# A two-layer decoder step: the mLSTM gates' scans moved into the first projection, and the mixer's start and the output projection's start reordered

## The chip, the core and the metric

The kernel runs on one core of one Trainium2 chip. The metric is the device time of one execution, in microseconds (us). The median of three runs of the kernel before is 2627.14 us (2625.72 to 2627.63). Profiled once, it took 2626.53 us.

## The reference, cut to what matters

Layer 0 has four mLSTM heads and four retention heads, each 256 wide, for a prompt of 1024 tokens and 8 sample sequences of 4 tokens ("samples"). One input projection gives q, k, v and a gate path z of every head, and for the mLSTM heads two scalars a token, ig and fg. Everything that the weights of a chunk need from these scalars depends on ig, fg and the old m alone:

```
p = h @ w_in
qk_m, v_m, z_m, ig, fg, q_r, k_r, v_r, z_r = split(p)
qk_c = silu(conv(buf0, qk_m))                  # conv_p, conv_s: the last rows
hm, C, n, m = mlstm_scan(q_m, k_m, v_m, ig + b_i, fg + b_f, C0, n0, m0)
    b = cumsum(log_sigmoid(fg))                # scans along the tokens
    Dm = b[t] - b[s] + ig[s];  m_t = maximum(b + m, max(Dm))
    w = exp(Dm - m_t)                          # weights of q k^T
    ws = exp(bL - b + ig - m_new);  sc = exp(bL + m - m_new)
hr, S = retention_scan(rope(q_r), rope(k_r), v_r, S0)
out = concat(rms(hm) * silu(z_m), rms(hr) * silu(z_r)) @ w_out
```

Layer 1 is differential attention, in stages that the change leaves alone.

## The kernel before

The program is a list of stages, each with one program per engine: norm, `project_layer0` (p0), `mix` (mx), `project_out_a` (oa), the second projection, attention and the last projection. Engines hand the memory over at a stage's end by the semaphores `left` and `cleared`.

**project_layer0** loops over 8 heads, mLSTM heads 0 to 3 and retention heads 4 to 7 (`head_loop`). For a head, TensorE (PE) computes four column tiles of q and k (`tile`, L572 to L574, about 11 us each) and the row blocks of v and z (`row_block`) in the order tile 0, tile 1, row block 1, tile 2, row blocks 2 and 3, tile 3, row blocks 4 to 8. Tile j lies in PSUM buffer j modulo 2, and PE takes a buffer again when `tile_taken` says so:

```
pe.wait_ge(tile_taken, m * 4 + (j + 1))        # tile(m, j)
dve.wait_ge(raw_ready, m * 4 + (2 * pair + 2)) # rotate(m, h, pair), heads 4 to 7
dve.sem_inc(tile_taken, 2)
```

ScalarE (ACT) copies a tile from PSUM (L680, L681), and VectorE (DVE) does the convolution of an mLSTM head or the rotation of a retention head (`rotate`, from L884 on). Results go to DRAM (`s_qk`, `s_v`, `s_g`) and come back in the mixer. Nearly all DMAs are issued by SyncE (SP), in the order of its program; it issues the next only when the queue has taken the last. The gate scalars (`s_gates`) are stored before the first head. The last rows of the convolution (`conv_p`, `conv_s`) are stored at the stage's end.

**mix** begins with the gates' chain (L1487 to L1522: scans on 4 partitions, by DVE, with an exponential and a logarithm of ACT within it, L1396 and L1398), then four exponentials (L1400 to L1402 and one more). PE turns the results into columns (L1229), spreads the samples' gates (L1237 to L1241), prepares the first chunk (`spread_m` L1249 and L1255, `turn_k` L1285, `scores` L1268), and then runs 8 chunks of 128 tokens, each with its products (`mx_num` L1311, L1340 to L1342) and one piece of the samples' work, beginning with `t_num(0)` (L1307), which needs the samples' values `t_v` and, for its later part, their state `t_state` (`load_t`). POOL clears the state (`mx_state`, L1469) and then signals `ready`, for which ACT and DVE wait and through them `gates_done`.

**project_out_a** multiplies the mixed rows by `w_out`. For the first row block b = 0, PE takes the 16 slices k one by one as ACT and DVE split them (`w_split`), and puts `project_few(k + 2)` (L1843, the samples' rows) between. For a row block it first turns the rows `oa_y` (`turn_y`, L1826). SP meanwhile has the final states to store (`store_states`: C_p, S_p, n_p, the last rows of `s_y`, n_s).

Of the kernel before, what the change touches and what calls it, by code (L numbers as in the profile page):

```python
# [31 lines left out]
P = 128  # L32
# [7 lines left out]
H = 4  # L40
# [329 lines left out]
def project_layer0(c, h_hi, h_lo, h_few):  # L370
# [9 lines left out]
    with Stage(c, "p0") as st:  # L380
# [50 lines left out]
        def head_loop(eng, body):  # L431

            with eng.Fori(0, H) as m:
                body(m, m, True)
            with eng.Fori(H, HEADS) as m:
                body(m, m - H, False)
# [38 lines left out]
        def sync(sp):  # L475
# [185 lines left out]
        def scalar(act):  # L661
# [36 lines left out]
            def body(m, h, mlstm):  # L698
# [5 lines left out]
                take_rows(m, 1)  # L704
                if mlstm:
                    sigmoid_exp(m, 1)
# [17 lines left out]
            head_loop(act, body)  # L724
# [69 lines left out]
        def vector(dve):  # L794
# [134 lines left out]
            head_loop(dve, body)  # L929
# [14 lines left out]
def mix(c, nxt):  # L944
# [8 lines left out]
    with Stage(c, "mx") as st:  # L953
# [12 lines left out]
        rows = st.sb("rows", [H, 2, NT], at=1664)  # L966
# [3 lines left out]
        t_q = st.sb("t_q", [P, 2, 2, DB, S], at=207488)  # L970
        t_w = st.sb("t_w", [S, 2, 4, S], at=211584)
        n_old = st.sb("n_old", [P, 2, S], at=212608)
        n_new = st.sb("n_new", [P, 2, S], at=212864)
        n_inc = st.sb("n_inc", [P, 2, S], at=213120)
        t_hn = st.sb("t_hn", [P, HH, VX], at=213376)
        places = {"late": 221600, "early": 162784}
# [6 lines left out]
        t_rep = little("t_rep", "late", [S, 2, P])  # L983
        n_out = st.sb("n_out", [S, DK], at=221600)
        select = little("select", "late", [H, H, P])
        junk = little("junk", "late", [P, 2, DK])
        n_rows = little("n_rows", "late", [S, DK])
        t_qw = little("t_qw", "late", [P, HH, S])
        mask = little("mask", "late", [P, P])
        t_wz = little("t_wz", "late", [P, HH, 2])  # L990
        t_wt = little("t_wt", "early", [S, HH, S])
# [3 lines left out]
        ws_rows = little("ws_rows", "early", [H, S])  # L995
# [14 lines left out]
        gates = st.sb("gates", [H, 2, NT], at=27264)  # L1010
        b = st.sb("b", [H, NT], at=35712)
        zeros = st.sb("zeros", [H, P], at=39936)
        ones = st.sb("ones", [H, P], at=40448)
        em = st.sb("em", [H, NT], at=10112)
        ws = st.sb("ws", [H, NT], at=14336)
        a = st.sb("a", [H, NT], at=20128)
        M = st.sb("M", [H, NT], at=92896)
        reset = st.sb("reset", [H, NT], at=121664)
        NCH = NB + DB
        small = {}  # L1020
        at = 18560
# [46 lines left out]

        def sync(sp):
# [69 lines left out]
            sp.wait_ge(gates_done, 1)  # L1139
# [85 lines left out]
        def tensor(pe):  # L1225
            pe.wait_ge(gr_dve, 2)
            for n in range(NB + 1):
                for q, x in ((A, a), (EM, em), (WS, ws)):
                    pe.transpose(pt[0:rows_of(n), (n * 3 + q) * H:(n * 3 + q + 1) * H],  # L1229
                                 x[:, n * P:n * P + rows_of(n)], c.ident[0:H, 0:H])  # L1230
            pe.matmul(pb[:, 0:2 * NCH * H], ones[:], diag[:].rearrange("h q n k -> h (q n k)"), start=True, stop=True).then_inc(gr_pe, 1)
            pe.wait_ge(gates_done, 1)
            pe.wait_ge(s_const, 32)
            pe.wait_ge(s_tconst, 16 * 13)
            for q, x in enumerate((rows[:, 0, T:NT], rows[:, 1, T:NT], ws_rows[:])):
                for h in range(H):
                    pe.matmul(bx[0][:, (q * H + h) * S:(q * H + h + 1) * S], select[:, h, :], x, start=True, stop=True)  # L1237
            pe.matmul(bx[1][:, 0:H], t_rep[:, 0, :], cols[0:S, NB, WS, :], start=True, stop=True)
            pe.matmul(bx[1][:, H:2 * H], t_rep[:, 1, :], cols[0:S, NB, EM, :], start=True, stop=True)
            for d in range(2):  # L1240
                last = pe.transpose(bx[1][:, 2 * H + d * S:2 * H + (d + 1) * S], n_rows[:, d * P:(d + 1) * P], c.ident[0:S, 0:S])  # L1241
            last.then_inc(t_spread, 1)
# [118 lines left out]
            scores(0, 1)  # L1361
            pe.wait_ge(t_wt_ready, 1)
# [31 lines left out]
        def scalar(act):  # L1394
# [3 lines left out]
            act.activation(b[:], b[:], ACT.Ln, bias=1.0).then_inc(gr_act, 1)  # L1398
            act.wait_ge(logs_ready, 2)
# [3 lines left out]
            act.activation(sc[:], sc[:], ACT.Exp).then_inc(gr_act, 1)  # L1403
            act.wait_ge(gates_done, 1)
# [34 lines left out]

            act.wait_ge(t_masked, 1)  # L1440
# [22 lines left out]
        def gpsimd(pool):  # L1463
# [9 lines left out]
            pool.wait_ge(gates_done, 1)  # L1473
            pool.wait_ge(gr_out, 32)
# [6 lines left out]
        def vector(dve):  # L1481
            ch = Chain(dve, dve_chain)
            dve.memset(inv[:], 1.0)
# [39 lines left out]
            dve.sem_inc(logs_ready, 1)  # L1523
            dve.wait_ge(gr_ws, 1)
# [116 lines left out]
            mask_m(0)  # L1641
            dve.wait_ge(s_tconst, 16 * 13)
# [73 lines left out]
def project_out_a(c, nxt):  # L1716
# [6 lines left out]
    with Stage(c, "oa") as st:  # L1723
# [266 lines left out]
        def vector(dve):  # L1990
# [51 lines left out]
            for k in range(2, KY):  # L2042
                split_w(k)
# [1533 lines left out]
```

## Time and profile before

| | before |
|---|---|
| median of 3 runs | 2627.14 us (2625.72 to 2627.63) |
| profiled execution | 2626.53 us, span 2624.6 us, mean granted TensorE clock 0.973 |
| busy: PE, DVE, ACT, POOL | 2484.1, 1309.5, 892.8, 408.2 us |
| PE's share of the chain that ended last | 87% |

The span is the time from the first to the last recorded instruction. An engine that is busy for 95% of it, as PE, bounds nearly every stage; the other 5% are gaps that lie at handovers.

### The profile page before, as it was taken

How to read it: one execution, taken by the hardware profiler on the slowest of the kernel's cores; microseconds unless marked ns; L12 is line 12 of the kernel's file. 1: busy time of each engine (PE TensorE's matmuls, PEld its weight loads, DVE VectorE, ACT ScalarE, POOL GpSimd, SP SyncE). 2: the span in 40 equal slices, each digit the busy share in tenths (PEclk: the TensorE clock that was granted, in tenths of full speed). 3: DMA queues.
4: the chain of work that ended last, by engine and by line, in shares of the span. 5: the costliest groups of instructions: out<-in, count | busy, mean ns of one | idle time of the engine just before them, and what ended most of it. 6: DMA issues, size and time to landing. Idle time of an engine off the chain costs nothing.

```text
span 2624.6 us, 47024 instructions
## 1 busy us (share of the span) xinstructions
PE 2484.1 (95%) x17168; PEld 1960.5 (75%) x17168; DVE 1309.5 (50%) x2214; ACT 892.8 (34%) x2136; POOL 408.2 (16%) x239
## 2 busy tenths in 40 slices
PE   7999999999993999979999999998999999999878
PEld 6898898888883777748878888875666666666557
DVE  4656555333333466652244343345666666666543
ACT  4222121111112333332132111145666666666521
POOL 4224223323400000000013232200000000000021
PEclk9999999999995999989999999999999999999989
DMA  5233223214217499882233335179999999999683
GB/s 160 78 109 105 81 80 116 77 59 128 81 69 207 121 290 282 273 266 91 86 108 108 97 95 141 58 244 393 403 390 406 402 391 394 407 398 390 252 242 97
DMA packets 333492, 536.73 MB, mean 205 GB/s; under 512 B 30117, under 2 KB 242866, under 8 KB 330074
## 3 DMA queue, kind: packets, MB, share of 16 engines
q1 hardware_dynamic: 330226, 525.47, 57.5%
q10 hardware_dynamic: 3080, 8.82, 0.9%
q8 instruction: 112, 1.84, 0.3%
q14 instruction: 74, 0.61, 0.1%
HBM read 432.86 MB, written 101.22 MB: 203 GB/s over the span
## 4 chain that ended last, share of the span: by engine, by line
PE 87%; DVE 4%; DMA 2%; issue 2%; SPq 2%; ACT 1%; ACTq 1%; POOL 0%; POOLq 0%; DVEq 0%
PE at_ring L2815 8%; PE p_col L572 5%; PE p_col L574 5%; PE p_col L573 5%; PE p_gm L2275 4%; PE p_gm L2276 4%; PE p_gm L2277 4%; PE at_ssc L2844 4%; PE at_ring L2833 4%; PE p_row L613 4%; PE p_row L615 4%; PE p_row L614 4%; PE at_sc L2783 3%; PE at_ring L2805 3%; PE oa_out L1833 2%; PE oa_out L1835 2%
## 5 line engine op out<-in xcount | busy, mean ns | idle before, releaser
L2815 PE MATMUL at_ring<-ident,at_kp 128*128 128x128 f32 x2048 | 268.6, 277 | 13.1 <-DMA at_kp<-in_cache_k 8.0
L2815 PEld LDWEIGHTS at_ring<-ident,at_kp 128*128 128x128 f32 x2048 | 224.0, 141 | 57.4 <-issue 37.5
L572 PE MATMUL p_col<-h_hi,p_wqk 128*128 128x352 f32 x768 | 251.3, 327 | 1.1 <-DVEq L801 1.1
L574 PE MATMUL p_col<-h_hi,p_wqk 128*128 128x352 f32 x768 | 247.3, 322 | 0.0
L573 PE MATMUL p_col<-h_lo,p_wqk 128*128 128x352 f32 x768 | 247.1, 322 | 0.0
L2916 ACT ACTIVATE at_kT<-at_ring 128x512 f32<-128x512 f32 x384 | 218.1, 596 | 70.4 <-PE at_ring L2815 68.4
L613 PE MATMUL p_row<-p_wvz,h_hi 128*128 128x512 f32 x512 | 203.8, 398 | 3.5 <-ACT p_vst L696 3.5
L2275 PE MATMUL p_gm<-p_whl,h_hi 128*128 128x512 f32 x512 | 202.6, 396 | 0.9 <-DVE h_lo L2415 0.6
L615 PE MATMUL p_row<-p_wvz,h_lo 128*128 128x512 f32 x512 | 202.1, 395 | 0.0
L614 PE MATMUL p_row<-p_wvz,h_hi 128*128 128x512 f32 x512 | 201.3, 393 | 0.0
L2276 PE MATMUL p_gm<-p_whl,h_hi 128*128 128x512 f32 x512 | 199.8, 390 | 0.0
L2277 PE MATMUL p_gm<-p_whl,h_lo 128*128 128x512 f32 x512 | 199.7, 390 | 0.0
L572 PEld LDWEIGHTS p_col<-h_hi,p_wqk 128*128 128x128 f32 x768 | 144.8, 188 | 7.3 <-issue 4.7
L573 PEld LDWEIGHTS p_col<-h_lo,p_wqk 128*128 128x128 f32 x768 | 144.9, 189 | 0.8
L574 PEld LDWEIGHTS p_col<-h_hi,p_wqk 128*128 128x128 f32 x768 | 145.0, 189 | 0.0
L2844 PE MATMUL at_ssc<-at_kT,at_qz 128*32 128x512 f32 x1024 | 123.5, 600 | 10.5 <-ACT at_alpha L2925 10.5
L3008 POOL TENSOR_TENSOR at_rstd<-at_o_ms,at_half 128x8 f32<-128x8 f32 x8 | 13.1, 1639 | 771.9 <-DVEq L3125 771.9
L3063 DVE COPY at_kT<-at_ring 128x512 f32<-128x512 f32 x128 | 88.4, 691 | 77.1 <-PE at_ring L2815 64.3
L2833 PE MATMUL at_ring<-at_vp,at_aT 128*32 128x256 f32 x2048 | 125.5, 386 | 0.7 <-ACT at_aT L2931 0.7
L827 DVE TENSOR_TENSOR p_ez<-p_vst,p_ez 128x256 f32<-128x256 f32 x64 | 41.4, 647 | 152.4 <-ACT p_vst L696 141.8
L2354 ACT ACTIVATE p_sig<-p_gm 128x128 f32<-128x128 f32 x64 | 17.7, 277 | 291.4 <-PE p_gm L2277 291.4
L613 PEld LDWEIGHTS p_row<-p_wvz,h_hi 128*128 128x128 f32 x512 | 96.3, 188 | 27.1 <-ACT p_vst L696 4.8
(403 smaller groups left out, 4872.1 us busy)
## 6 DMA issues: line engine op xcount, KB each, us to landing
at_kp<-in_cache_k SPq DMA_DIRECT2D x256, 512.0 KB, 7.6
at_vp<-in_cache_v SPq DMA_DIRECT2D x256, 512.0 KB, 7.5
s_qk<-p_res SPq DMA_DIRECT2D x32, 528.0 KB, 2.8
p_wst<-in_w_in_a SPq DMA_DIRECT2D x32, 512.0 KB, 3.9
p_wst<-in_w_in_a SPq DMA_DIRECT2D x64, 256.0 KB, 2.9
mx_qk<-s_qk SPq DMA_DIRECT2D x16, 1024.0 KB, 9.5
p_wst<-in_w_in_c SPq DMA_DIRECT2D x64, 256.0 KB, 4.6
s_v<-p_vst SPq DMA_DIRECT2D x64, 128.0 KB, 2.9
```

The source lines that it names most:

```text
L572: pe.matmul(out[:, r, 0:TN], wx[:, 0, k, :], h_hi[:, k, at], start=k == 0, stop=False)
L573: pe.matmul(out[:, r, 0:TN], wx[:, 0, k, :], h_lo[:, k, at], start=False, stop=False)
L574: last = pe.matmul(out[:, r, 0:TN], wx[:, 1, k, :], h_hi[:, k, at], start=False, stop=k == KD - 1)
L613: pe.matmul(row[:, i % 2, :], h_hi[:, k, at], wvz[:, 0, k, :], start=k == 0, stop=False)
L614: pe.matmul(row[:, i % 2, :], h_hi[:, k, at], wvz[:, 1, k, :], start=False, stop=False)
L615: last = pe.matmul(row[:, i % 2, :], h_lo[:, k, at], wvz[:, 0, k, :], start=False, stop=k == KD - 1)
L2275: pe.matmul(out, c.h_hi[:, k, at_b], whl[s][:, 0, k, :], start=k == 0, stop=False)
L2276: pe.matmul(out, c.h_hi[:, k, at_b], whl[s][:, 1, k, :], start=False, stop=False)
L2277: last = pe.matmul(out, c.h_lo[:, k, at_b], whl[s][:, 0, k, :], start=False, stop=k == KD - 1)
L2815: last = pe.transpose(bank("key", n, f)[:, h * PAGE:(h + 1) * PAGE], kp[n % 2][k][:, tile:tile + P], c.ident[:])
L2833: last = pe.matmul(bank("val", n, 0)[32 * j:32 * j + 32, 0:256], aT[:, n % 2, k, 32 * j:32 * j + 32], v[:, :, j, :], start=k == 0, stop=k ...
L2844: last = pe.matmul(ssc[32 * j:32 * j + 32, :], qz[:, n // NGB, j, i, :], kT[:, n % 2, j + JC * i, :], start=i == 0, stop=i == 1)
```

## The change

Three places change. In p0, between head 3 and head 4, SP stores the convolution's rows, waits for these stores and issues the five loads of the gates' chain; DVE runs the whole chain there (`gates_between`), ACT its exponential and logarithm ahead of head 4 and its four exponentials behind row block 1 of head 4. In mx, what is left of the gates is PE's turning into columns; the first chunk's preparation comes next, and the samples' gates are spread behind it, in `spread_samples`; the loads are reordered. In oa, SP issues the states' stores and the second `oa_y` load ahead of nine small loads, and PE runs all `project_few` ahead of b = 0. The two stores of the convolution and their wait leave p0's end. The chain's buffers share places in SBUF, and POOL's memset of `t_y` waits for nothing any more.

```diff
@@ project_layer0, sync @@
             head(H - 1, H - 1, False, (0, True))
+            sp.wait_ge(tail_saved, 4 * H)
+            sp.dma_start(c.out["conv_p"][0, 0], tail_rows[0:NR, :]).then_inc(s_end, 16)
+            sp.dma_start(c.out["conv_s"].rearrange("a b r n -> (a b r) n"),
+                         tail_rows[NR:NR + DB * NR, :]).then_inc(s_end, 16)
+            sp.wait_ge(gates_stored, 16)
+            sp.wait_ge(s_end, 32)
+            c.mx.load_gates(sp)
             with sp.Fori(H, HEADS - 1) as m:
...
-            sp.wait_ge(tail_saved, 4 * H)
-            sp.dma_start(c.out["conv_p"][0, 0], tail_rows[0:NR, :]).then_inc(s_end, 16)
-            sp.dma_start(c.out["conv_s"].rearrange("a b r n -> (a b r) n"),
-                         tail_rows[NR:NR + DB * NR, :]).then_inc(s_end, 16)
             sp.wait_ge(s_end, 32)
@@ project_layer0, scalar @@
                 take_rows(m, 1)
+                if first:
+                    c.mx.scalar_weights(act)
...
-            head_loop(act, body)
+            with act.Fori(0, H) as m:
+                body(m, m, True)
+            c.mx.scalar_logs(act)
+            body(H, 0, False, True)
+            with act.Fori(H + 1, HEADS) as m:
+                body(m, m - H, False)
@@ project_layer0, vector @@
-            head_loop(dve, body)
+            def gates_between(dve):
+                dve.wait_ge(s_end, 32)
+                c.mx.vector_gates(dve)
+
+            head_loop(dve, body, gates_between)
@@ mix, sync @@
             load_qk(0, 0)
+            sp.dma_start(kout[:], c.tab["kout"]).then_inc(s_late, 16)
+            load_qk(0, 1)
...
+            load_t(0)
             for r in range(4):
                 sp.dma_start(t_v[32 * r:32 * r + 32, :, 0:DK], c.s_v[T:NT, :].rearrange("t (h n) -> t h n", h=HH)).then_inc(s_tconst, 16)
-            load_t(0)
-            load_qk(0, 1)
             load_v(0)
@@ mix, tensor @@
-            pe.wait_ge(gr_dve, 2)
+            pe.wait_ge(gr_ws, 1)
...
             scores(0, 1)
+            spread_samples()
             pe.wait_ge(t_wt_ready, 1)
             t_turn(0)
@@ project_out_a, sync @@
+            c.mx.store_states(sp)
+            load_y(1)
             sp.dma_start(fold[:], c.tab["fold"]).then_inc(s_tab, 16)
...
-            load_y(1)
-            c.mx.store_states(sp)
@@ project_out_a, tensor @@
-            project_few(0)
+            for k in range(4):
+                project_few(k)
             c.mx.turns_free(pe)
             turn_y(0, 0)
-            project_few(1)
+            for k in range(4, 8):
+                project_few(k)
             turn_y(0, 1)
+            for k in range(8, KY):
+                project_few(k)
...
-                            if k + 2 < KY:
-                                project_few(k + 2)
                             pe.wait_ge(w_split, k + 1)
```

DVE between the last row block of head 3 (L829) and the rotation of head 4 (L884), before:

```order
L829 TENSOR_TENSOR p_gst<-p_ez,p_gnb 128x256 [waits stage1_36]
L433 REGISTER_ALU [waits stage1_39]
L433 COMPARE_AND_BRANCH
L435 UNCONDITIONAL_BRANCH
L877 ISA [waits stage1_1]
L884 SCALAR_TENSOR_TENSOR p_acc<-p_raw,p_cos 128x1024 [waits stage1_18]
L884 SCALAR_TENSOR_TENSOR p_acc<-p_raw,p_cos 128x32
L884 SCALAR_TENSOR_TENSOR p_acc<-p_raw,p_sin 128x1024
```

and with the change (`p_` buffers are of p0, `mx_` ones of the mixer's chain; the rotation is L895 there):

```order
L1514 SCALAR_TENSOR_TENSOR mx_b<-mx_gates 4x1056 [waits stage0_7,cleared0,stage1_38]
L1516 MEMSET mx_zeros 4x128 [waits stage0_63]
L1518 SCALAR_TENSOR_TENSOR mx_gates<-mx_gates,mx_b 4x1056 [waits stage0_2,stage0_63]
L1520 SCALAR_TENSOR_TENSOR mx_b<-mx_rows,mx_gates 4x1056 [waits stage0_0,stage0_63]
L1521 TENSOR_TENSOR mx_gates<-mx_gates,mx_b 4x1056 [waits stage0_63]
L1523 COPY mx_ext<-mx_mp 4x8 [waits stage0_63]
...
L1547 TENSOR_TENSOR mx_gates<-mx_gates,mx_ml 4x32 [waits stage0_63]
L1549 TENSOR_TENSOR mx_sc<-mx_mp,mx_ml 4x16 [waits stage0_63]
L888 ISA [waits stage1_1]
L895 SCALAR_TENSOR_TENSOR p_acc<-p_raw,p_cos 128x1024 [waits stage1_18]
```

The 44 instructions of the chain now stand between the two heads, and the rotation behind them. SP at the same place, behind the last stores of head 3, with the change (before, L473 followed L502 at once):

```order
L504 DMA s_g<-p_gst 128x256 [waits stage1_29]
L544 DMA out_conv_p<-p_tail_rows 3x2048 [waits stage1_25]
L545 DMA out_conv_s<-p_tail_rows 24x2048
L1083 DMA mx_gates<-s_gates 4x2112 [waits cleared0,stage1_38,stage1_14]
L1084 DMA mx_rows<-tab_reset 4x1056
L1085 DMA mx_first<-tab_first 4x40
L1086 DMA mx_ones<-tab_ones 4x128
L1087 DMA mx_mp<-in_state_mlstm_m 4x8x1
...
L475 ISA [waits stage1_26]
L475 DMA p_wst<-in_w_in_a 128x4x256
```

The two stores and five loads stand ahead of the weights of the next heads. PE at the mixer's start, from the last turned gate columns (`mx_prep<-ident`) on, before:

```order
L1229 MATMUL mx_prep<-ident,mx_ws 32x4
L1231 MATMUL mx_bk<-mx_diag,mx_ones 128x128
L1237 MATMUL mx_x<-mx_rows,mx_select 128x32 [waits stage0_13,stage0_11,stage0_8]
L1237 MATMUL mx_x<-mx_ws_rows,mx_select 128x32 x4
L1239 MATMUL mx_x<-mx_cols,mx_t_rep 128x4
L1241 MATMUL mx_x<-ident,mx_n_rows 128x32 x2
L1249 MATMUL mx_prep<-mx_rows,mx_select 128x128 [waits stage0_29]
L1285 MATMUL mx_bk<-ident,mx_qk_119 128x128 [waits stage0_15]
L1268 MATMUL mx_prep<-mx_qk_119 128x128 [waits stage0_31,stage0_15]
```

and with the change:

```order
L1243 MATMUL mx_prep<-ident,mx_gates 32x4
L1246 MATMUL mx_bk<-mx_diag,mx_ones 128x128 [waits stage0_1]
L1267 MATMUL mx_prep<-mx_rows,mx_select 128x128 [waits stage0_29,stage0_11,stage0_8]
L1303 MATMUL mx_bk<-ident,mx_qk_119 128x128 [waits stage0_15]
L1286 MATMUL mx_prep<-mx_qk_119 128x128 [waits stage0_31,stage0_15]
...
L1286 MATMUL mx_prep<-mx_qk_119 128x128 [waits stage0_36,stage0_17]
L1255 MATMUL mx_x<-mx_rows,mx_select 128x32 [waits stage0_13]
L1255 MATMUL mx_x<-mx_ws_rows,mx_select 128x32 x4
L1257 MATMUL mx_x<-mx_cols,mx_t_rep 128x4
L1259 MATMUL mx_x<-ident,mx_n_rows 128x32 x2
L1311 MATMUL mx_bk<-ident,mx_t_qk 32x128 [waits stage0_41,stage0_51]
```

The samples' gates (`mx_x<-mx_rows,mx_select`) moved behind the second scores (L1286). SP's loads at the mixer's start, before:

```order
L1074 DMA mx_qk_119<-s_qk 128x16x128
L1114 DMA mx_t_qk<-s_qk 128x32x32
L1115 DMA mx_t_rep<-tab_spread_s 32x256
...
L1122 DMA mx_t_idle<-tab_idle_rows 128x1
L1124 DMA mx_t_v<-s_v 32x8x256 x4
L1097 DMA mx_t_state_129<-in_state_mlstm_C 128x8x256 x2
L1074 DMA mx_qk_119<-s_qk 128x16x128
L1080 DMA mx_vx_127<-s_v 128x8x256
L1128 DMA mx_kout<-tab_kout 128x4
L1129 DMA mx_decay<-tab_decay 128x512
```

and with the change:

```order
L1094 DMA mx_qk_119<-s_qk 128x16x128
L1129 DMA mx_kout<-tab_kout 128x4
L1094 DMA mx_qk_119<-s_qk 128x16x128
L1131 DMA mx_decay<-tab_decay 128x512
L1132 DMA mx_gin<-tab_gin 128x512
L1133 DMA mx_t_qk<-s_qk 128x32x32
L1134 DMA mx_t_rep<-tab_spread_s 32x256
...
L1141 DMA mx_t_idle<-tab_idle_rows 128x1
L1117 DMA mx_t_state_129<-in_state_mlstm_C 128x8x256 x2
L1144 DMA mx_t_v<-s_v 32x8x256 x4
L1100 DMA mx_vx_127<-s_v 128x8x256
```

The second half of qk and the decay tables are now ahead of the samples' constants, and the samples' state ahead of `mx_t_v`. In oa, SP before:

```order
L1104 DMA out_S_s<-mx_t_state_130 128x8x256
L1797 DMA oa_fold<-tab_fold 128x32
L1800 DMA oa_few_post<-in_norm_post 32x256
L1801 DMA oa_few_res<-in_x_sample 32x256
...
L1801 DMA oa_few_res<-in_x_sample 32x256
L1788 DMA oa_y<-s_y 128x2048 [waits stage1_25]
L1179 DMA out_C_p<-mx_state 128x4x256 [waits stage0_45]
L1179 DMA out_S_p<-mx_state 128x4x256 x2
L1182 DMA out_n_p<-mx_state 128x4x1 x2
L1185 DMA s_y<-mx_y_138 128x2048 [waits stage0_48]
```

and with the change:

```order
L1124 DMA out_S_s<-mx_t_state_130 128x8x256
L1193 DMA out_C_p<-mx_state 128x4x256 [waits stage0_45]
L1193 DMA out_S_p<-mx_state 128x4x256 x2
L1196 DMA out_n_p<-mx_state 128x4x1 x2
L1199 DMA s_y<-mx_y_138 128x2048 [waits stage0_48]
L1201 DMA out_n_s<-mx_n_out 32x256 [waits stage0_60]
L1820 DMA oa_y<-s_y 128x2048 [waits stage1_25]
L1831 DMA oa_fold<-tab_fold 128x32
L1834 DMA oa_few_post<-in_norm_post 32x256
```

The states' stores and `oa_y` moved ahead of `oa_fold` and the eight loads behind it.

## Rows read from the trace of the kernel before

**Rows 1.** Windows of two stretches: start and end, length, busy (instructions) of each engine.

```profile
core 0: us, PE busy (x) PEld busy (x) DVE busy (x) ACT busy (x) POOL busy (x), PEclk, DMA share, GB/s
420.00:450.00 30.00, 30.00 (x224) 27.29 (x223) 9.93 (x10) 4.04 (x13) 12.08 (x7) 1.00 0.32 93
830.00:834.60 4.60, 0.00 (x0) 0.00 (x0) 1.20 (x7) 3.13 (x4) 0.00 (x0) 0.50 1.16 309
```

**Rows 2.** Chain that ended last, 795 to 870 us: start, length, engine, work.

```profile
798.17 1.88 DMA s_g<-p_gst
800.49 2.48 DMA out_conv_s<-p_tail_rows
803.11 2.59 DMA mx_gates<-s_gates
805.73 1.26 DVE mx_b L1487
...
830.69 0.17 DVE mx_sc L1522
...
834.66 2.77 PE mx_prep L1229 x27
...
838.73 5.32 PE mx_x L1237 x24
...
845.12 1.87 PE mx_prep L1249 x8
...
859.35 0.70 DVE mx_wt L1551
...
863.15 0.92 PE mx_num L1307 x8
```

**Rows 3.** Timeline of SP's DMA issues at the mixer's start.

```profile
808.18 4.36 SPq L1115 DMA_DIRECT2D mx_t_rep<-tab_spread_s  x1
...
816.14 2.70 SPq L1124 DMA_DIRECT2D mx_t_v<-s_v  x4
```

**Rows 4.** Windows of the DMA queues at the mixer's start (last columns: clock, DMA share, GB/s).

```profile
821.00:822.50 1.50, 0.50 1.11 195
824.00:825.50 1.50, 0.50 1.09 351
```

**Rows 5.** Timeline of POOL at the mixer's start.

```profile
804.73 3.52 POOL L1469 MEMSET mx_state<- 128x4112 f32 x1
```

**Rows 6.** Timeline of SP between heads 3 and 4.

```profile
436.99 0.39 SPq L502 DMA_DIRECT2D s_g<-p_gst  x1
```

**Rows 7.** Timeline of DVE at head 4 (in brackets the idle time before, and its end).

```profile
445.62 1.23 DVE L884 SCALAR_TENSOR_TENSOR p_acc<-p_raw,p_cos 128x1024 f32<-128x1024 f32 x1 [19.71 <-ACT p_raw L681]
```

**Rows 8.** Timeline of PE at head 4, tile 2.

```profile
449.22 0.32 PE L572 MATMUL p_col<-h_hi,p_wqk 128*128 128x352 f32 x1
```

**Rows 9.** Chain that ended last, 1100 to 1190 us.

```profile
1139.18 4.02 SPq L1797
...
1153.48 2.56 SPq L1182
1156.09 12.78 DMA out_n_p<-mx_state
```

**Rows 10.** Timeline of PE in b = 0 of oa.

```profile
1143.02 0.50 PE L1833 MATMUL oa_out<-oa_w_hi,oa_yT 128*128 128x512 f32 x1
...
1171.39 0.79 PE L1833 MATMUL oa_out<-oa_w_hi,oa_yT 128*128 128x512 f32 x1 [3.63 <-DVE oa_w_lo L1996]
...
1181.26 0.39 PE L1833 MATMUL oa_out<-oa_w_hi,oa_yT 128*128 128x512 f32 x1
...
1182.63 1.03 PE L1826 MATMUL oa_turn<-ident,oa_y 128*128 128x128 f32 x8
```

**Rows 11.** Windows of PE behind that gap.

```profile
1172.00:1177.00 5.00, 5.00 (x18) 0.50 0.27 111
```

**Rows 12.** Windows of the DMA queues in oa.

```profile
1161.50:1163.00 1.50, 1.00 0.40 16
```

More of the change, by code:

```diff
@@ L428, in rows_at, with head_loop @@
             return slice((i - 1) * P, i * P)
-        def head_loop(eng, body):
+        def head_loop(eng, body, between=None):
             with eng.Fori(0, H) as m:
                 body(m, m, True)
+            if between:
+                between(eng)
             with eng.Fori(H, HEADS) as m:
@@ L969, in mix @@
         t_kw = st.sb("t_kw", [P, 2, 2, DK], at=203392)
[L970 to L976, printed above, removed]
+        t_q = st.sb("t_q", [P, 2, 2, DB, S], at=1664)
+        t_w = st.sb("t_w", [S, 2, 4, S], at=5760)
+        n_old = st.sb("n_old", [P, 2, S], at=6784)
+        n_new = st.sb("n_new", [P, 2, S], at=7040)
+        n_inc = st.sb("n_inc", [P, 2, S], at=7296)
+        t_hn = st.sb("t_hn", [P, HH, VX], at=217088)
+        places = {"late": 225536, "early": 162784}
         def little(name, zone, shape):
@@ L1008, in mix @@
         bk = st.ps("bk", [P, 512])
[L1010 to L1018, printed above, removed]
+        gates = st.sb("gates", [H, 2, NT], at=217088)
+        b = st.sb("b", [H, NT], at=191104)
+        zeros = st.sb("zeros", [H, P], at=195328)
+        ones = st.sb("ones", [H, P], at=195840)
+        a, ws, em = gates[:, 0, :], gates[:, 1, :], b
+        M, reset = rows[:, 0, :], rows[:, 1, :]
         NCH = NB + DB
         small = {}
-        at = 18560
+        at = 196352
         for name, n in (("first", DB * (DS + 1)), ("ext", DB * (DS + 1)), ("mext", DB * (DS + 1)), ("mp", NCH + 1), ("ml", NCH), ("bl", NCH),
@@ L1066, in by_chunk, with load_gates @@
             return x[:, 0:T].rearrange("h (n t) -> h n t", t=P) if prompt else x[:, T:].rearrange("h (n t) -> h n t", t=DS)
+        def load_gates(sp):
+            sp.wait_ge(c.cleared[0], 1)
+            sp.dma_start(gates[:].rearrange("h q t -> h (q t)"), c.s_gates).then_inc(s_gates, 16)
+            sp.dma_start(reset[:], c.tab["reset"]).then_inc(gr_in, 16)
+            sp.dma_start(first[:], c.tab["first"].rearrange("h (b t) -> h b t", b=DB)).then_inc(gr_in, 16)
+            sp.dma_start(ones[:], c.tab["ones4"]).then_inc(gr_in, 16)
+            sp.dma_start(mp[:, NB:NCH], c.x["state_mlstm_m"][0].rearrange("b h -> h b"), allow_slow_non_contiguous=True).then_inc(gr_in, 16)
         def sync(sp):
@@ L1233, in tensor, with spread_samples @@
             pe.wait_ge(s_const, 32)
[L1234 to L1242, printed above, removed]
+            def spread_samples():
+                pe.wait_ge(s_tconst, 16 * 13)
+                for q, x in enumerate((rows[:, 0, T:NT], rows[:, 1, T:NT], ws_rows[:])):
+                    for h in range(H):
+                        pe.matmul(bx[0][:, (q * H + h) * S:(q * H + h + 1) * S], select[:, h, :], x, start=True, stop=True)
+                pe.matmul(bx[1][:, 0:H], t_rep[:, 0, :], cols[0:S, NB, WS, :], start=True, stop=True)
+                pe.matmul(bx[1][:, H:2 * H], t_rep[:, 1, :], cols[0:S, NB, EM, :], start=True, stop=True)
+                for d in range(2):
+                    last = pe.transpose(bx[1][:, 2 * H + d * S:2 * H + (d + 1) * S], n_rows[:, d * P:(d + 1) * P], c.ident[0:S, 0:S])
+                last.then_inc(t_spread, 1)
             def spread_m(n):
@@ L1438, in take_t_num @@
                 act.activation(junk[:, use % 2, :], bnum[use % 2][:, 0:DK], ACT.Square, accum_out=t_ssq[:, j:j + 1]).then_inc(num_taken, 1)
+            weights(0)
+            for i in range(2):
+                take_k(0, i)
+            act.wait_ge(s_late, 48)
+            for i in range(2, 4):
+                take_k(0, i)
             act.wait_ge(t_masked, 1)
@@ L1479, in gpsimd, with vector_gates @@
                 pool.tensor_tensor(fac2[:], fac[:], half[:], ALU.pow).then_inc(fac_rooted, 1)
-        def vector(dve):
+        links = []
+        def vector_gates(dve):
             ch = Chain(dve, dve_chain)
-            dve.memset(inv[:], 1.0)
+            links.append(ch)
+            dve.wait_ge(c.cleared[0], 1)
             f = gates[:, 1, :]
@@ L1523, in vector @@
             dve.sem_inc(logs_ready, 1)
+        def vector(dve):
+            ch = links[0]
+            dve.memset(inv[:], 1.0)
             dve.wait_ge(gr_ws, 1)
@@ L2043, in vector @@
                 split_w(k)
+            dve.wait_ge(gcol_turned, 1)
+            ch.link(dve.tensor_copy(gcol[:], back[:, 1, 3 * P:3 * P + KD]))
+            dve.sem_inc(back_free, 1)
             c.mx.rows_free(dve)
```

58 lines of the change are left out of this document (23 added, 35 removed).

## The prediction

> **What bounds the kernel now.** The table first: PE is busy for 95% of the span, so the only time to be had lies where PE waits. I then read the windows of a stretch of p0 and of the mixer's start. In p0 PE is busy for 30.00 of 30 us, but at the mixer's start, from 830.00 to 834.60, for nothing, at a clock of 0.50 [rows 1]. The chain of waits names what PE waits for there: s_g's store, the convolution's stores, the gates' loads, then DVE's chain from 805.73 on, ACT's exponentials, and PE at 834.66 [rows 2]. Nothing hides this chain, and it stands there only by the program's order: its inputs (s_gates) are stored before the first head. So it can go where DVE has spare time. In p0 DVE is busy for 9.93 of 30 us [rows 1], and it is idle for 19.71 us before head 4's rotation [rows 7]. The question is whether the chain fits where it is put, since there too it runs ahead of something.
>
> **Part A: the mixer's start gains.** I count from T0, when the loads behind p0's end are issued: 803.11 before [rows 2]. s_g's last store lands at 798.17 + 1.88 = 800.05; the convolution's stores, which landed at 800.49 + 2.48 = 802.97, are gone [rows 2]. T0 moves by 2.9 us. From T0 to t_num(0) it took 863.15 - 803.11 = 60.0 us.
> With the change PE turns the gate columns at once (2.77 us), to T0 + 4. POOL's memset of the state, 3.52 us, began 1.6 us after T0 [rows 5] and binds next: the first spreading begins at T0 + 5.4. From there to the end of the second scores took 859.35 - 845.12 = 14.2 us [rows 2], so they end at about T0 + 20. Then `spread_samples` waits for all 13 sample loads, the last of them t_v. Its time follows from SP's queue. Ahead of it now stand qk's first half and second half (1.05 MB each), the decay tables (0.5 MB), t_qk, the samples' constants and the state (2.1 MB). Before, t_rep's issue (4.36 us) ended at 812.54, T0 + 9.4, and t_v's began at 816.14, 3.6 us later [rows 3]. At the 195 and 351 GB/s of [rows 4] the second half of qk adds 3.0 to 5.4 us and the tables 1.5 to 2.7, but part of that hides under t_rep's 4.36 us of blocked issue; I add 3.7, so t_rep's issue ends near T0 + 13.1 and the small loads' near T0 + 16.7. The state takes 2.1 MB / 351 GB/s = 6.0 us, to T0 + 23 to 24; t_v, 1.05 MB at 195 GB/s, 5.4 us, to about T0 + 29.5 [rows 4]. Behind it the spreading takes 845.12 - 838.73 = 6.4 us [rows 2], to T0 + 36; then the samples' weights and turning up to t_num(0) take 863.15 - 859.35 = 3.8 [rows 2], and 0.6 for ACT's exponential: T0 + 40.7. So A = 60.0 - 40.7 + 2.9 = 22.2 us, and I take off 0.7 because PE stands idle for 9 us behind the scores and begins again at half clock: **A = 21.5**. Its bounds: were t_v there at T0 + 20, t_num(0) would come at T0 + 31 and A be 32; with t_v at T0 + 33, A is 18.
>
> **Part B: the seam in p0 costs.** SP issues head 3's last store at 436.99 and is through at 437.38 [rows 6]; it cannot come to the gates' loads earlier, since they stand behind it. From s_g's landing at 800.05 to DVE's first operation at 805.73 the same steps (convolution's stores, wait, loads) took 5.7 us [rows 2]: DVE begins at 443.1. The chain takes 830.69 + 0.17 - 805.73 = 25.1 us, ACT's two operations in it [rows 2]: it ends at 468.2. DVE's rotation of head 4, which began at 445.62 [rows 7], stands behind it, and `tile_taken`, which this rotation gives at its start, lets PE take the buffer of tile 2. PE began that tile at 449.22 [rows 8], so only 3.6 us of the delay are covered. It now begins at 468.6: a gap of 19.4 us. ACT waits in its program as well, with head 4's copies behind it, but only for the chain's first part; it makes them up while DVE scans on. After such a gap PE is slow: behind the gap of 3.63 us in oa it began again at 1171.39 and ran at 0.50 up to 1177.00 [rows 10, 11], 5.6 us at half speed, which cost 2.8 us. I add 2.5: **B = 21.9**, between 19.4 (no cold start) and 24.5 (the chain 2 us longer beside ACT's table loads). Nothing gives it back: PE is busy for all of the 30 us around it [rows 1] and bounds the heads behind. That DVE had 19.71 us of idle time [rows 7] doesn't help, for it ends where the chain begins: the idle time is from 425.9 to 445.6.
> The four exponentials of ACT (3.1 us) stand behind row block 1, with PE 11 us away in the next tile: nothing. The memset of t_y on POOL is off the path: nothing. Head 4's weights are issued 5.7 us later on SP, which is less than the gap: nothing.
>
> **Part C: oa.** Before, SP was in fold's issue from 1139.18 to 1143.20 and came to n_p at 1153.48; n_p's second store landed at 1156.09 + 12.78 = 1168.87 and only then could ACT split slice 11, for which PE waited 3.63 us [rows 9, 10]. Now C_p and S_p follow S_s directly. At 351 GB/s [rows 4] their 2.1 MB take 6 us behind S_s's and land near 1153. n_p's packets are 4 bytes: in their stretch the queues moved 16 GB/s [rows 12] for about 6 us, to 1159. So slice 11 is free at 1159 instead of 1168.9, and this stall goes. PE meanwhile runs the 14 `project_few` that stood in b = 0 ahead of it, partly in idle time, and b = 0 begins between 1143.02 [rows 10] and some 1153 (I take 1148); a slice without the few takes 1182.63 - 1181.26 = 1.4 us [rows 10]. After 8 slices, at 1159.2, PE turns oa_y(1). This load now stands behind n_p and the 1 MB store of s_y: two transfers of 1.05 MB at 351 GB/s are 6.0 us, so it lands near 1165. That is a new stall of 5.8 us. Then cold clock 2.5, turning 1.9 and 8 slices at 1.40: 1165 + 2.5 + 1.9 + 11.2 = 1180.6, against 1182.63 before [rows 10]: **C = 2.0**. If oa_y(1) weren't late, it would be 1159.2 + 1.0 + 11.2 = 1171.4 and C = 11; if it landed at 1170, C = -3.
> The Trainium skill ("DMA: Bandwidth & Descriptors", section "Queues, rings and completion order") says that each DMA engine consumes the descriptors of a queue in ring order. By this rule a load that moves behind n_p's small packets waits for them on every engine, as I have it; without it C would be 11.
>
> **The sum.** Against the profiled execution of 2626.5: 2626.5 - 21.5 + 21.9 - 2.0 = 2624.9. The median of runs stands 0.6 above the profiled execution, so 2625.5.
>
> **The rivals.** A run of this kernel tells a change of about 0.2% (5.3 us) from none.
> *It cancels* (my forecast, 0.50): the chain has moved from one place where PE waits for it to another. 2625.5, by itself 2622 to 2632.
> *The mixer or oa gives more* (0.28). For it: t_v and oa_y(1) are small loads whose landing I only estimate, and both wait behind transfers whose rates vary between 195 and 351 GB/s [rows 4]. With A = 27 or C = 11 it is 2626.5 - 27 + 21.9 - 5 = 2616; against it: SP's queue was blocked in just these places [rows 3, 9].
> *The seam is hidden* (0.07). If DVE's chain were done before PE needs tile 2's buffer, B would be under 3 and the time 2606. For it speaks DVE's idle time [rows 7]; against it that SP has the gates' loads behind head 3's last store [rows 6], so that it needs a chain under 6 us.
> *The samples come too late* (slower, 0.15). t_v is behind 5.3 MB where 1.05 MB stood before. One mechanism: each load waits in SP's queue until the queue takes it, as t_rep did for 4.36 us [rows 3]. Were the state's issue to block for as long again and t_v land at T0 + 40, then t_num(0) comes at T0 + 51 and A is 11: 2626.5 - 11 + 21.9 - 2 = 2635. The point from which it decides is t_v at about T0 + 37. Against it: t_v lies behind what the rates in [rows 4] carry in 23 us.
>
> **How the numbers follow.** The predicted time is the forecast's. The range reaches down to the second case (2614) and leaves out the hidden seam; upward it takes in most of the last case, to 2634. Faster by over 0.2% (under 2621.9): 0.28 + 0.07 = 0.35. Slower (over 2632.4): 0.15, and the forecast's own tail, 0.03. Same: 0.50 - 0.03 = 0.47.
>
> **What would show it.** Right: DVE's chain in p0 from 443 to 468 and a gap of PE of about 19 us before tile 2 of head 4; at the mixer's start no chain, but a wait of PE behind the scores that t_v's landing ends, and t_num(0) 22 us nearer to p0's end; in oa, no wait for n_p and one for oa_y(1). Wrong: the chain much shorter or longer than 25 us, or PE idle elsewhere in head 4; t_v there before the scores end, or after T0 + 37; oa_y(1) there by 1159.

## The result, and the profile after

The change made the kernel slower: 2631.11 us (median of 13 runs, 2627.36 to 2635.2) against 2624.89 us (13 runs, 2622.14 to 2627.63), a ratio of 1.0024 with an interval of 1.0017 to 1.0032. I had forecast 1.6 us less than the profiled execution of before. The profiled execution of the changed kernel took 2627.36 us and is the fastest of the 13, so the path is read from marks within it and not from its end. I name the changed kernel "after".

**The seam in p0.** The chain that ended last, of after, 437 to 450 us (start, length, engine, work):

```profile
437.55 0.32 SPq L544
437.92 2.73 DMA out_conv_s<-p_tail_rows
440.71 2.56 DMA mx_gates<-s_gates
443.40 1.26 DVE mx_b L1514
```

The timeline of after around it, DVE's last operation of the chain and its rotation, and then PE's tile 2:

```profile
468.36 0.16 DVE L1549 TENSOR_TENSOR mx_sc<-mx_mp,mx_ml 4x16 f32<-4x16 f32 x1
469.13 1.33 DVE L895 SCALAR_TENSOR_TENSOR p_acc<-p_raw,p_cos 128x1024 f32<-128x1024 f32 x2 [0.60 <-DVE mx_sc L1549]
...
469.09 0.66 PE L576 MATMUL p_col<-h_hi,p_wqk 128*128 128x352 f32 x1 [19.66 <-DVEq L889]
```

These rows show the predicted order with its times: the convolution's stores right behind the last store of head 3, the gates, DVE from 443.40 to 468.52, the rotation behind it, and PE idle for 19.66 us ahead of the tile that began at 449.22 before [rows 7, 8]. The last s_g store of p0 lands at 822.44 instead of 800.05 [rows 2]: B = 22.4 in this execution.

**The mixer's start.** The chain of after from SP's t_v issues on:

```profile
841.58 2.09 SPq L1144
843.72 10.75 DMA mx_t_v<-s_v
854.51 5.33 PE mx_x L1255 x24
...
865.33 1.08 PE mx_num L1325 x8
```

No chain of DVE stands here any more. PE waits for t_v, which lands at 854.47, 31.8 us after T0 (822.69); I had put it at 29.5. t_num(0) comes at T0 + 42.6 instead of T0 + 60.0 [rows 2]; with the 2.8 us that the convolution's stores took, A = 63.1 - 42.9 = 20.2 us, both counted from s_g's landing.

**The output projection.** The absolute times of the two profiles can't be compared here, since after comes to this stage later. I count from F, the start of the samples' rows (timeline of PE, before and after):

```profile
1128.79 1.34 PE L1874 MATMUL oa_turn<-ident,oa_x 32*128 32x32 f32 x16
...
1131.91 1.91 PE L1906 MATMUL oa_turn<-ident,oa_x 32*128 32x32 f32 x16
```

SP's timeline of after, its states' stores and oa_y(1):

```profile
1135.90 6.01 SPq L1124 DMA_DIRECT2D out_S_s<-mx_t_state  x2
1141.96 6.93 SPq L1193 DMA_DIRECT2D out_C_p<-mx_state  x2
1148.93 2.71 SPq L1193 DMA_DIRECT2D out_S_p<-mx_state  x2
1151.68 2.96 SPq L1196 DMA_DIRECT2D out_n_p<-mx_state  x2
1154.68 1.46 SPq L1199 DMA_DIRECT2D s_y<-mx_y  x1
...
1156.66 3.32 SPq L1820 DMA_DIRECT2D oa_y<-s_y  x1
```

and what ACT and PE waited for (timeline, in brackets the idle time and its end):

```profile
1167.92 4.84 ACT L1954 ACTIVATE oa_w_hi<-oa_w_raw 128x1024 fp32r<-128x1024 f32 x5 [11.18 <-DMA out_n_p<-mx_state]
...
1173.16 1.97 PE L1858 MATMUL oa_turn<-ident,oa_y 128*128 128x128 f32 x8 [14.49 <-DMA oa_y<-s_y]
1187.06 1.03 PE L1858 MATMUL oa_turn<-ident,oa_y 128*128 128x128 f32 x8
```

n_p was issued at F + 19.8, 4.9 us earlier than before (F + 24.7), and released slice 11 at F + 36.0 instead of F + 40.1 [rows 9]. C_p's two issues took 6.93 us here. oa_y(1) landed 16.5 us after its issue, at F + 41.2, and PE waited 14.49 us for it. The last row answers to 1182.63 of [rows 10]: at this mark after is 4.4 us late, 3.1 of which it had already at F. From F to this mark it took 55.15 us, in before 53.84.

### The profile page after: what moved, and what is told of

Same layout as the page of the kernel before. It is cut to its first block, busy times and chain, and to the rows that moved or that the text cites. A ratio compares the mean times of both kernels' runs of the same rounds, so it can differ in the third digit from the quotient of the medians.

```text
span 2625.3 us, 47003 instructions
## 1 busy us (share of the span) xinstructions
PE 2479.5 (94%) x17168; PEld 1964.4 (75%) x17168; DVE 1311.3 (50%) x2214; ACT 896.5 (34%) x2139; POOL 409.6 (16%) x239
## 4 chain that ended last, share of the span: by engine, by line
PE 86%; DVE 4%; DMA 3%; SPq 3%; issue 2%; ACT 1%; ACTq 1%; POOL 0%; POOLq 0%; DVEq 0%
PE at_ring L2848 8%; PE p_col L576 5%; PE p_col L578 5%; PE p_col L577 5%; PE p_gm L2308 4%; PE p_gm L2310 4%; PE p_gm L2309 4%; PE at_ssc L2877 4%; PE at_ring L2866 4%; PE p_row L617 4%; PE p_row L619 4%; PE p_row L618 4%; PE at_sc L2816 3%; PE at_ring L2838 3%; PE oa_out L1865 2%; PE oa_out L1867 2%
## 5 line engine op out<-in xcount | busy, mean ns | idle before, releaser
L2877 PE MATMUL at_ssc<-at_kT,at_qz 128*32 128x512 f32 x1024 | 121.8, 593 | 10.8 <-ACT at_alpha L2958 10.8
L838 DVE TENSOR_TENSOR p_ez<-p_vst,p_ez 128x256 f32<-128x256 f32 x64 | 40.1, 626 | 151.5 <-ACT p_vst L700 140.9
```

The costliest lines, as they stand in the source:

```text
L2877: last = pe.matmul(ssc[32 * j:32 * j + 32, :], qz[:, n // NGB, j, i, :], kT[:, n % 2, j + JC * i, :], start=i == 0, stop=i == 1)
```

## The experiments

Ratios are to the kernel before, which ran beside each of them on the same chip. "H" is the version of the run seam_hidden.

**after_again** is after, without an edit.

> The changed kernel itself, unchanged, for a second profile beside the others. Its first profile was the fastest of 13 executions, 0.8 us above the profile of before, where the medians stand 6.2 us apart. Theory (the loss is fixed in place: seam +22.4, mixer's start -20.2, output projection +1.8, together +4.0): the marks up to the second turned half of row block 1 in the output projection lie again at +4.4 us (1187 us), and the rest varies from run to run by some us. Rival (a part behind that, the second projection or attention, is systematically slower): the marks there lie later than before by more than 4.4 us. Ratio to before 1.001 to 1.003.

Measured: 2629.62 us, ratio 1.0021 (1.0012 to 1.003). The last mark came at 1185.79, and from there to the end of the span it took 1441.2 us, before 1442.0, in after 1438.2. So after's one profile was 3 us lucky behind the marks, in stages that the change leaves alone, and the loss is in place ahead of them. These two and oa_old (below) run the same p0, and their gap is nearly the same (19.66, 19.80 and 19.96 us), but T0 is 822.69, 821.44 and 825.63. Windows of PE behind the gap, first after, then after_again, then oa_old:

```profile
471.00:473.00 2.00, 2.00 (x8) 0.50 0.00 0
473.00:475.00 2.00, 2.00 (x10) 0.66 0.00 0
475.00:477.00 2.00, 2.00 (x14) 1.00 0.08 34
...
500.00:530.00 30.00, 28.35 (x135) 1.00 0.22 71
```

```profile
471.00:473.00 2.00, 2.00 (x8) 0.53 0.00 0
473.00:475.00 2.00, 2.00 (x15) 1.00 0.00 0
475.00:477.00 2.00, 2.00 (x14) 1.00 0.67 266
```

```profile
471.00:473.00 2.00, 2.00 (x8) 0.50 0.00 0
473.00:475.00 2.00, 2.00 (x9) 0.50 0.00 0
475.00:477.00 2.00, 2.00 (x12) 0.80 0.00 0
...
500.00:530.00 30.00, 28.20 (x130) 0.95 0.22 71
```

The granted clock is the number behind the brackets. PE began again at 469.09, 467.99 and 470.03, and by these windows the clock was at half until about 474.4, 472.9 and 475.8. That is 5.3, 4.9 and 5.8 us at half, which cost 2.6, 2.4 and 2.9 us: the clock behind the gap differs little. The rest of the spread lies elsewhere: PE came to the gap at 449.43, 448.19 and 450.07, and in oa_old the clock fell once more, from about 527 to 530 and shortly behind a wait of 1.80 us for ACT, which cost 1.5 us (0.95 over 30 us); behind the same wait in after, 1.65 us there, it stayed at 1.00. Over the three, B is 22.4, 21.1 and 25.3 against the one profile of before, in the mean 23.0. In the eleven profiles whose p0 has no such gap (before and ten of the runs below) s_g's last landing lies between 798.6 and 800.4; against their mean, 799.5, B is 23.5.

**seam_hidden (H)**: the chain's place in head 4.

```diff
@@ project_layer0, vector: body of head 4 @@
                     rotate(m, h, 0)
-                    z_rows(m, h, range(0, 4))
+                    z_rows(m, h, range(0, 2))
+                    if first:
+                        gates_between(dve)
+                    z_rows(m, h, range(2, 4))
@@ scalar: body of head 4 @@
                 take_rows(m, 1)
                 if first:
-                    c.mx.scalar_weights(act)
+                    c.mx.scalar_logs(act)
...
                 take_rows(m, 4)
+                if first:
+                    c.mx.scalar_weights(act)
-            c.mx.scalar_logs(act)
             body(H, 0, False, True)
```

> The changed kernel, with the gates' chain of DVE put behind row blocks 0 and 1 of head 4 instead of ahead of its rotation, ACT's exponential and logarithm behind row block 1 and its four exponentials behind row block 4. Theory (the loss in p0 is the wait of PE's tile 2 for the rotation that gives tile_taken, and DVE is idle from about 456 to 484 us but for two row blocks): PE has no gap over 1 us in head 4, the chain runs from 456 to 482, and p0 ends 22 us earlier than in the changed kernel; ratio to before 0.9935 to 0.996. Rival (25 us of scans hold something else of head 4, the z rows or the copies of ACT behind its table loads): a gap of 5 to 20 us at tile 3 or row block 4 remains; ratio 0.997 to 1.002.

Measured: 2607.71 us, ratio 0.9935 (0.9921 to 0.9948). The timeline of DVE, first and last operation of the chain and the z rows behind it:

```profile
454.86 1.25 DVE L1522 SCALAR_TENSOR_TENSOR mx_b<-mx_gates 4x1056 f32<-4x1056 f32 x1 [0.26 <-DVE p_gst L841]
...
479.81 0.16 DVE L1557 TENSOR_TENSOR mx_sc<-mx_mp,mx_ml 4x16 f32<-4x16 f32 x1
480.20 0.42 DVE L839 TENSOR_TENSOR p_ez<-p_vst,p_ez 128x256 f32<-128x256 f32 x1 [0.23 <-DVE mx_sc L1557]
```

and the window of head 4 in this run:

```profile
440.00:500.00 60.00, 59.11 (x317) 52.02 (x315) 43.30 (x76) 19.85 (x35) 10.44 (x5) 1.00 0.19 63
```

The same 25 us of scans, 11 us later, cost PE next to nothing: it is busy for 59.11 of 60 us, in before for 60.00. T0 comes at 799.06 instead of 822.69, and the median lies 21.9 us below after_again's. The theory of the seam holds, and the rival falls. (The edit moves ACT's two parts of the chain too; that it was the rotation that held PE is read from after's trace.)

**oa_old** and **hidden_oa_old**: the output projection as before, in after and in H.

```diff
@@ project_out_a, sync @@
-            c.mx.store_states(sp)
-            load_y(1)
             sp.dma_start(fold[:], c.tab["fold"]).then_inc(s_tab, 16)
...
+            load_y(1)
+            c.mx.store_states(sp)
@@ tensor @@
-            for k in range(4):
-                project_few(k)
...
+                            if k + 2 < KY:
+                                project_few(k + 2)
```

> The changed kernel with the whole part of the change in the output projection undone (SP's order, PE's few products, the copy of gcol). Theory (that part loses about 2 us, because oa_y(1) now lands late): oa from its first weights to the second turned half of row block 1 is 2 us shorter than in the changed kernel, ratio to before about 1.0015. Rival (that part gains, and the loss is in the mixer's end): ratio over 1.0024, the n_p wait is back and costs more than oa_y(1) does.

> The seam's chain hidden as in the run seam_hidden, and the output projection as before. Theory: both losses are gone, what is left is the gain at the mixer's start: 20 us, ratio to before 0.992 to 0.9935, a version faster than both kernels. Rival (as for seam_hidden): 0.996 to 1.0.

Measured: 2630.0 us, 1.0024 (1.0015 to 1.0033), and 2610.13 us, 0.9946 (0.9932 to 0.9959). Beside after_again (2629.62) and H (2607.71) no difference can be told, and "both losses gone" was too much. With the old order the wait for n_p at slice 11 is back, 6.08 us in oa_old and 3.40 in hidden_oa_old, and the wait for oa_y(1) is gone. A third run put the same part alone on the kernel before.

**oa_only**: before, with the change's part in project_out_a, which is the reverse of the diff above.

> The kernel before with nothing but the change's part in the output projection. The prediction gave it a gain of 2.0 us. By the marks of the runs so far (from t_num(0) to the second turned half of row block 1: 321.5 to 322.8 us with the new order, 320.7 and 321.9 with the old one in the changed mixer, 319.5 before) it costs 0 to 2 us: ratio to before 1.000 to 1.001. Rival (the prediction's): 0.999.

Measured: 2624.38 us, ratio 1.0004 (0.9995 to 1.0013). From F to the last mark it took 55.25 us, in before 53.84: 1.4 us more. The prediction had 2.0 less, which the interval of the ratio (1.3 us less to 3.4 us more) leaves out. How large the loss is, one profile doesn't tell: the old order took 53.84, 55.06 (oa_old) and 54.97 us (hidden_oa_old), the new one 55.15, 54.78, 57.09 (H), 55.25 and 55.29 (tv_first). The means lie 0.9 us apart, less than the profiles of one order do, so that the gain of 2.0 is ruled out and a small loss is likely, but not shown.

This run says something of part A as well, since its p0 and its mixer are those of before. From s_g's landing to t_num(0) it took 60.97 us, in before 63.10. The same first and second scores took 3.08 and 1.80 us of PE instead of 3.76 and 3.21: before's clock came back later. Against the mean of the two A is 19 us and not 20.2.

**tv_first**: H with t_v ahead of the samples' state.

```diff
-            load_t(0)
             for r in range(4):
                 sp.dma_start(t_v[32 * r:32 * r + 32, :, 0:DK], ...)
+            load_t(0)
             load_v(0)
```

> The version of the run seam_hidden, with the samples' values t_v loaded ahead of their state (load_t(0)) at the mixer's start. In seam_hidden t_num(0) comes 43 us after the loads behind p0 begin, and PE waits for t_v alone behind the scores. Theory (t_v's landing sets t_num(0), and 2.1 MB of state ahead of it delay it by about 6 us): t_v lands 6 us earlier, t_num(0) comes 5 to 6 us earlier, ratio to before 0.9912 to 0.992. Rival (t_v's small rows are slow by themselves, or the state binds next in its place): the state's products wait instead, and under 2 us are won, 0.993.

Measured: 2597.99 us, ratio 0.9899 (0.9884 to 0.9915). The chain of this run at the mixer's start, which begins at 799.79:

```profile
818.29 5.77 DMA mx_t_v<-s_v
824.11 5.33 PE mx_x L1263 x24
...
834.93 1.08 PE mx_num L1333 x8
```

t_v lands at T0 + 24.3 instead of about T0 + 32, and t_num(0) comes at T0 + 35.1, in H at T0 + 42.9: 7.7 us, a little more than expected. PE doesn't wait for the state in this trace.

**y_mid**, **y_first**, **n_first**: H with another order on SP in oa.

```diff
@@ y_mid: store_states, S_p, then @@
+            load_y(1)
             n_p's two stores
@@ y_first @@
+            load_y(1)
             c.mx.store_states(sp)
-            load_y(1)
@@ n_first: y_first, and in store_states @@
+            n_p's two stores
             C_p's and S_p's four stores
-            n_p's two stores
```

> The version of seam_hidden, with oa_y(1) loaded between the stores of S_p and n_p, so behind C_p and S_p (2.1 MB) but ahead of n_p's 4-byte packets and s_y's last MB. In seam_hidden PE waits 14.9 us for oa_y(1), which lands about 16.5 us after its issue. Theory (the small packets of n_p hold what stands behind them): oa_y(1) lands 10 to 14 us earlier and the wait for it is under 3 us; PE then waits for n_p at slice 11 instead, so that of these some 4 to 5 us are won, ratio 0.9915 to 0.992. Rival (the queue is full of C_p and S_p, and the small packets cost little): oa_y(1) lands at most 4 us earlier, and the ratio stays at 0.993.

> The version of seam_hidden, with oa_y(1) loaded ahead of all of the states' stores. Theory (as for y_mid): no wait for oa_y(1), PE waits at slice 11 for n_p, which lands some 3 us later than in seam_hidden, so it gains about as much as y_mid or 1 to 2 us less. Rival (C_p and S_p are what holds oa_y(1)): y_first gains 4 us or more above y_mid.

> The version of y_first, with n_p's two stores ahead of C_p's and S_p's. Theory (n_p's 4-byte packets take their own 12 us or so, whatever is ahead, and C_p and S_p can move beside them): all six stores have landed by about 1158 us minus the 22 us that the seam gave back, slice 11 waits for under 3 us, and b = 0 ends 10 us or more earlier than in seam_hidden; ratio 0.989 to 0.990. Rival (C_p and S_p behind the small packets wait for them on every DMA engine): the last of the six lands as late as in y_first, and the ratio is that of y_first.

Measured: 2601.84 us, 0.9913 (0.9898 to 0.9928); 2602.27 us, 0.992 (0.9907 to 0.9934); 2599.59 us, 0.9906 (0.989 to 0.9921). From F to the last mark: H 57.1 us, y_mid 49.5, y_first 49.5, n_first 47.2. All gain, though about 2 us of it is that H's profile is the slowest of its order. The times of the three can't be told apart. But in y_mid oa_y(1), though ahead of n_p, still landed 15.7 us after its issue; PE waited 9.0 us for it:

```profile
1145.70 1.97 PE L1867 MATMUL oa_turn<-ident,oa_y 128*128 128x128 f32 x8 [9.00 <-DMA oa_y<-s_y]
```

So the expected landing failed, and the gain was larger than expected all the same. y_first's theory came out in part: PE doesn't wait for oa_y(1), but 7.59 us for slice 11. n_first's theory fell: with n_p ahead of them C_p's and S_p's stores took 12 to 13 us from issue to landing (9 to 12 in y_first), and the last of the six released slice 11 at 1145.41, F + 36.2, in y_first at F + 37.8; the wait for it was 5.72 us and not under 3.

**no_n_p** and **y_mid_no_n_p**: H and y_mid without the two stores of n_p, whose output is left out.

> The version of seam_hidden without the two stores of n_p (that output is left out, all else is computed). Theory (n_p's 4-byte packets hold the queue for 7 to 10 us and what stands behind them waits): oa_y(1), which stands behind them there, lands 6 to 9 us earlier against its issue (in seam_hidden 17.6 us after it), slice 11 waits for C_p and S_p alone and hardly at all; the second turned half of row block 1 comes 10 to 14 us earlier. Rival (C_p, S_p and s_y, 3.1 MB, are what holds it): oa_y(1) lands under 3 us earlier.

> The version of y_mid without the two stores of n_p (that output is left out). In y_mid oa_y(1) was issued ahead of n_p and still landed 15.7 us after its issue. Theory (small packets behind a load hold it too, since the engines reach them before all of the load's packets are through): it lands 8 to 10 us after its issue. Rival (it was only the bytes ahead, C_p and S_p): 14 to 16 us as in y_mid.

Measured: 2600.21 us, 0.9903 (0.9887 to 0.992), and 2591.56 us (one run). oa_y(1) lands 10.8 us after its issue in no_n_p, in H 17.6; and 10.4 in y_mid_no_n_p, in y_mid 15.7. The same row as above, without n_p:

```profile
1137.51 1.09 PE L1864 MATMUL oa_turn<-ident,oa_y 128*128 128x128 f32 x8 [2.97 <-DMA oa_y<-s_y]
```

The two stores of n_p, 2 KB each in 4-byte packets, cost a load behind them 6.8 us and a load ahead of them 5.3 us. The other orders agree with the second: with n_p issued right behind it oa_y(1) took 15.7 us (y_mid), 14.8 (n_first) and 16.5 (best), and 11.8 with C_p's and S_p's 2.1 MB between them (y_first). One more reading comes from no_n_p: S_p, with no n_p behind it, released slice 11 at F + 26.9, 6.0 us after S_s had released its slice at F + 20.9 (timeline of ACT). The windows of the queues in y_mid show the stretch in which little moves (last column GB/s):

```profile
1134.00:1137.00 3.00, 1.00 1.04 373
1137.00:1140.00 3.00, 0.84 2.17 149
1140.00:1143.00 3.00, 0.50 0.29 16
1143.00:1146.00 3.00, 0.50 0.81 158
```

**best**: H with t_v first, oa_y(1) first, and n_p ahead of C_p and S_p.

> The hidden seam with all that the runs before it favour: t_v ahead of the samples' state, oa_y(1) ahead of all states' stores, n_p ahead of C_p and S_p. Theory (the three gains lie at three places of PE's path and add): 7 us of t_v and 10 us of the output projection's start below seam_hidden, ratio to before 0.9865 to 0.9885. Rival (one of them is given back in the other's place): not under 0.989.

Measured: 2591.78 us, ratio 0.9875 (0.9857 to 0.9893), 33 us below before, and 39 below the median of after. The timeline of PE, the two turns of row block 1 in oa:

```profile
1129.35 1.09 PE L1866 MATMUL oa_turn<-ident,oa_y 128*128 128x128 f32 x8 [1.27 <-DMA oa_y<-s_y]
1148.36 1.04 PE L1866 MATMUL oa_turn<-ident,oa_y 128*128 128x128 f32 x8
```

47.2 us from F (1101.17) to the last mark, and t_num(0) at 834.58: both gains are there together.

## Why the prediction was wrong

**Part A held but for a size.** Predicted 21.5, measured 20.2 in these two profiles, and 19 with oa_only's mixer taken in. The step that was off is t_v's landing: "to about T0 + 29.5", measured T0 + 31.8. I let t_v's transfer begin when the state's was through at 351 GB/s and gave it 5.4 us; in fact its last issue took until T0 + 21.0 and the landing another 10.75 us. The sum had a slip too: 29.5 + 6.4 + 3.8 + 0.6 is 40.3 and not 40.7, and the 0.7 us for the half clock behind the wait was not needed, for the spreading took 6.4 us as before. These two made the miss smaller than t_v's 2.3 us. That it is t_v that PE waits for, and the state ahead of it that makes it late, tv_first showed.

**Part B held.** Predicted 21.9, measured 22.4 in after and 23.0 to 23.5 in the mean of three profiles. The gap (19.4 predicted, 19.66 measured), its place and its cause, the rotation's `tile_taken` behind the chain, are as described, and with the chain behind the rotation, in seam_hidden, the loss was gone. The 2.5 us for the half clock, sized from one restart, measured 2.4 to 2.9; what varies between the three profiles is mostly not this.

**Part C failed, and this is the step with which the forecast failed.** Predicted was a gain of 2.0; measured is a loss of about 1 us, 1.4 in oa_only's profile and 0.9 in the means of eight. The prediction's times are on the clock of before, where F is 1128.79; measured ones below are put on that clock. "At 351 GB/s their 2.1 MB take 6 us behind S_s's and land near 1153", and from it "slice 11 is free at 1159". The rate held and the start did not: S_s released its slice only at 1149.9 (timeline of ACT, before),

```profile
1149.87 3.90 ACT L1921 ACTIVATE oa_w_hi<-oa_w_raw 128x1024 fp32r<-128x1024 f32 x4 [1.89 <-DMA out_S_s<-mx_t_state]
```

and some 6 us behind that is 1155.7, where S_p lands in no_n_p, 2.7 us later than I had it. From there to n_p's landing I had 6 us, and it took 9. So slice 11 was free at 1164.8 and not at 1159, and oa_y(1), which I rightly had some 6 us behind it (5.2 measured), landed at 1170.0 and not at 1165. PE, which had finished its eight slices at 1155.6 instead of 1159.2, waited 14.5 us for it where I had 5.8. The prediction itself said that a landing at 1170 would turn the gain into a loss, of 3 us; it was less, because the stretch from the landing to the mark took 13.9 us and not 15.6. The rule of the Trainium skill that I drew on ("DMA: Bandwidth & Descriptors", section "Queues, rings and completion order") points the right way, as no_n_p shows for the load behind; it doesn't explain y_mid, where a load ahead of the small packets is late too. Why that is stays open, since no row here shows the packets engine by engine.

**The sum.** In the profile of after 22.4 - 20.2 + 1.3 is 3.5, and 0.9 us lie between t_num(0) and F: 4.4, what its last mark shows. (That stretch, which nothing changes, takes from 265.6 to 267.0 us in all profiles.) By the means of all profiles it is 23.5 - 19 + 0.9, some 5.4; the medians stand 6.2 apart, with an interval of 4.5 to 8.4. The forecast was -1.6. Of the 6.0 us between it and the mark of after 3.3 are C, 1.3 are A, 0.5 is B and 0.9 the scatter behind t_num(0). Two terms of some 20 us cancel to almost nothing here, so that misses of 1 to 3 us decide the sign. Of the rivals none came out as told. The slower one put its mechanism in t_v at T0 + 37; t_v came at T0 + 31.8, and the loss was made of small misses with one sign. That 2625.5 looks only 5.6 us off is luck in part: the three first runs of before, on which it stands, had a median 2.2 us above that of the 13.

**The rest.** POOL's memset, the four exponentials and the later weights of head 4 were rightly costed at nothing: apart from the gap PE waits only for ACT's copies of row blocks, 3.4 us in three pieces from 440 to 800 us, before 3.5. That moving the chain to where "DVE is idle" doesn't help by itself is the case's main point, and it was right: the idle time that counts lies 11 us behind.

## What to carry to other kernels

From this case: a chain of small operations is moved under a matrix stage behind the point at which its engine has released what TensorE needs next; look for the engine's idle time that follows a release, not for the idle time that ends in one. When a load is moved in an in-order queue, count the bytes that stand ahead of it and not the issues, and keep stores in packets of a few bytes away from loads that something waits for, on either side. Count times from a mark at the stage's start, since two profiles come to it at different times. And when terms of 20 us are to cancel, one profile of each kernel is too few: here the same unchanged stretches differed by 1 to 2 us from one profile to the next.

## What the runs showed that I had not expected

Behind the same gap of about 20 us PE stood at half clock for 4.9, 5.3 and 5.8 us in three executions. Behind a wait of 1.8 us later in the stage it fell again in one of them (oa_old) and not in the other two. The mixer's start of one and the same program took 63.10 and 60.97 us in two profiles, and the difference is in how long the scores ran at the slower clock. The 13 runs of after lie 7.8 us apart, those of before 5.5; but 21 further runs of before, beside after_again, lie 11.5 apart, so that the spread can't be put down to the gap. And two stores of 2 KB in 4-byte packets delayed not only the load behind them (6.8 us) but a 1 MB load that had been issued 1.3 us ahead of them (5.3 us, one profile each).
